# Moving the split weights by 32 bytes in each partition of SBUF

## The reference

```python
proj = h @ w_in[l]
...
x = x + mixed @ w_out[l]
...
up = h @ w_up
...
return (jax.nn.gelu(gate) * val) @ w_down
...
u = h @ w_in
...
y = y + gates[:, :, n] * (branches[n] @ w_branch[n])
return y @ w_out
```

## Time and profile before

| | |
|---|---|
| Median of 3 runs | 3691.65 us |
| Span of the profiled execution | 3692.1 us |
| TensorE matmul busy | 3530.3 us (96%), 28202 matmuls |
| TensorE weight load busy | 3442.9 us (93%) |
| VectorE busy | 2005.9 us (54%) |
| ScalarE busy | 1877.3 us (51%) |
| Mean granted TensorE clock | 0.980 of full speed |
| HBM read | 580.12 MB, 158 GB/s |

### The profile page before, as it was taken

The page is one execution under the profiler, slowest core; times in us unless marked ns, Lnnn a source line. Parts: engine busy times, 40 slices in busy tenths (PEclk is TensorE's granted clock), DMA queues, the critical chain, the costliest instruction groups (busy, mean ns, idle before and its releaser), DMA issues.

```text
span 3692.1 us, 74435 instructions
## 1 busy us (share of the span) xinstructions
PE 3530.3 (96%) x28202; PEld 3442.9 (93%) x28202; DVE 2005.9 (54%) x3133; ACT 1877.3 (51%) x2994; POOL 142.5 (4%) x159
## 2 busy tenths in 40 slices
PE   8999699999999998999999999998999999999999
PEld 7888699999999997899899999998899999999999
DVE  5666445555555545556544555555566644555554
ACT  4444635535534444655545764444565555773443
POOL 0000000000000003000000100000000000110000
PEclk8999899999999998999999999999999999999999
DMA  4223344555555543344345435553434345444554
GB/s 156 103 91 127 109 161 171 182 181 173 182 180 180 182 162 130 121 148 151 130 171 192 173 136 186 188 189 139 140 141 152 135 156 194 171 152 171 184 192 148
DMA packets 89888, 584.03 MB, mean 158 GB/s; under 512 B 10400, under 2 KB 10784, under 8 KB 27552
## 3 DMA queue, kind: packets, MB, share of 16 engines
q1 hardware_dynamic: 88272, 577.54, 44.1%
q0 software_dynamic: 1488, 4.72, 0.4%
HBM read 580.12 MB, written 2.10 MB: 158 GB/s over the span
## 4 chain that ended last, share of the span: by engine, by line
PE 56%; ACT 2%; issue 2%; DVE 1%; DVEq 0%; DMA 0%; ACTq 0%; SPq 0%
PE bank L180 17%; PE bank L182 17%; PE bank L181 17%; PE m L1982 1%; ACT w_hi L156 1%; PE m L1969 1%; PE m L2001 0%; PE m L2010 0%; PE m L234 0%; DVE tn L256 0%; PE m L1984 0%; PE m L2046 0%; PE m L1991 0%; PE m L2012 0%; PE m L2011 0%
## 5 line engine op out<-in xcount | busy, mean ns | idle before, releaser
L161 DVE TENSOR_TENSOR w_lo<-raw,w_hi 128x768 fp32r<-128x768 f32 (+5 forms) x1202 | 1346.4, 1129 | 1047.4 <-ACT w_hi L156 1045.3
L180 PE MATMUL bank<-h,w_hi 128*128 128x256 f32 x5808 | 1677.6, 289 | 45.9 <-DVE h L263 25.4
L181 PE MATMUL bank<-h,w_hi 128*128 128x256 f32 x5808 | 1653.6, 285 | 0.0
L182 PE MATMUL bank<-h,w_lo 128*128 128x256 f32 x5808 | 1653.4, 285 | 0.0
L156 ACT ACTIVATE w_hi<-raw 128x768 fp32r<-128x768 f32 (+5 forms) x1202 | 1107.5, 972 | 167.2 <-PE bank L182 163.7
L180 PEld LDWEIGHTS bank<-h,w_hi 128*128 128x128 f32 x5808 | 1124.8, 194 | 57.3 <-issue 31.6
L181 PEld LDWEIGHTS bank<-h,w_hi 128*128 128x128 f32 x5808 | 1125.9, 194 | 3.0 <-issue 1.4
L182 PEld LDWEIGHTS bank<-h,w_lo 128*128 128x128 f32 x5808 | 1124.7, 194 | 0.0
L180 PE MATMUL bank<-mid,w_hi 128*128 128x256 f32 x1376 | 395.5, 287 | 9.1 <-DVE mid L1930 6.1
L182 PE MATMUL bank<-mid,w_lo 128*128 128x256 f32 x1376 | 386.3, 281 | 0.0
L181 PE MATMUL bank<-mid,w_hi 128*128 128x256 f32 x1376 | 384.9, 280 | 0.0
(11 more groups left out here) (350 smaller groups left out, 3229.7 us busy)
## 6 DMA issues: line engine op xcount, KB each, us to landing
raw<-in_w SPq DMA_DIRECT2D x485, 1024.0 KB, 4.8
raw<-in_w_br SPq DMA_DIRECT2D x96, 512.0 KB, 4.2
raw<-in_w_uq SPq DMA_DIRECT2D x8, 768.0 KB, 4.3
raw<-in_w_ukv SPq DMA_DIRECT2D x8, 512.0 KB, 3.3
bias_t<-in_bias POOLq DMA_DIRECT2D x16, 192.0 KB, 2.9
x<-in_x SPq DMA_DIRECT2D x4, 512.0 KB, 6.5
raw<-in_w_kr SPq DMA_DIRECT2D x4, 512.0 KB, 3.5
out_x<-x SPq DMA_DIRECT2D x1, 2048.0 KB, 6.4
```

The costliest lines, as they stand in the source:

```text
L161: dve.tensor_tensor(w_lo[:, b % 2, c], raw[:, b, c], w_hi[:, b % 2, c].bitcast(F32), ALU.subtract).then_inc(S["lo_done"], 1)
L180: pe.matmul(o, w_hi[:, b % 2, c], a_hi, start=start and k == t0, stop=False)
L181: pe.matmul(o, w_hi[:, b % 2, c], a_lo, start=False, stop=False)
L182: last = pe.matmul(o, w_lo[:, b % 2, c], a_hi, start=False, stop=stop and k == t0 + nt - 1)
```

## The change

Four small tensors are declared that nothing reads or writes. `w_offset` (8 floats, 32 bytes) stands ahead of `w_hi`, `x_offset` (24 floats, 96 bytes) ahead of `x`, and 32 bytes stand ahead of `mixed` and of `mid`. No instruction is added, removed or moved.

```diff
         raw = sb("raw", [4, UNIT])
+        w_offset = sb("w_offset", 8)
         w_hi = sb("w_hi", [2, UNIT], F32R)
         w_lo = sb("w_lo", [2, UNIT], F32R)
+        x_offset = sb("x_offset", 24)
         x = sb("x", [KT, SEQ])
         h = sb("h", [KT, 2 * SEQ], F32R)
...
+        mixed_offset = buf("mixed_offset", 8)
         mixed = buf("mixed", [KT, 2 * SEQ], F32R)
...
+        mid_offset = buf("mid_offset", 8)
         mid = buf("mid", [KT, 2 * SEQ], F32R)
```

## The result

The changed kernel takes 3698.24 us against 3694.03 us for the kernel before (medians of 20 runs each): 1.0015 times, with a 95% interval of 1.0008 to 1.0021. By this ratio it is 0.15% slower, inside what the prediction called no change; 1.2% faster had been forecast. One of the 20 runs of before took 19335.59 us, which nothing here explains; the median does not hang on it. The profiled execution spans 3692.2 us, that of before 3692.1 us, but it is among the faster of its kernel: 3694.61 us, where the 20 runs go from 3693.86 to 3702.94.

The account below looks back on a forecast made before the run. Matmul cost on TensorE was taken to bound the kernel. Savings of 15.2 + 28.2 + 2.1 = 45.5 us, less 0.45 us to the median, took 3692.1 to 3646.1 us, 1.2% faster; range 3624 to 3712 us.

Parts of the forecast that it names:

- What bounds the kernel: Whole kernel: matmuls under way in 96% of the span, so a change in one matmul's cost goes nearly whole into time.
- (a): `h` matmuls, 32 bytes from the weights, fall from 120.0 ns: 15.2 us in feed-forward, 28.2 us elsewhere after the first stage.
- rival 2: Moving operand's own start decides: `h` stays at 120.0 ns, `mixed` and `mid` rise to it, 18 us slower; chance 0.15.
- (b): First stage: cheaper `h` matmuls save 2.1 us, half of the 4.3 us there to be had.
- (c): `mixed` and `mid` matmuls: distance to the weights stays +32 bytes, so 0; bounds 6 us less, 18 us more.
- (d): Weights starting 32 past a multiple of 64 are not dearer by themselves: 0, though up to 3.3 ns could be hidden.
- (e): Splits on ScalarE and VectorE: about 0 from the new alignment, at most 1%, 15 ns, hidden by slack.
- (f): What comes next: loads already keep the faster pace; swapped alignment of small buffers costs 2 us at most either way.
- Rival 1: Buffer's place in memory decides, so 32 bytes change nothing: 3691 to 3692 us; no-change chance 0.20, shared.
- Rival 3: Sign of the distance counts: `h` stays at 120.0 ns (no-change chance 0.20, shared) or reaches 3748 us (0.06).
- rival 4: Weights off a multiple of 64 free more: `h` at 115 ns, 94 us saved, 3598 us; chance 0.06.
- The rule against the change: TensorE's two independent SBUF read ports mean operand distance can't matter, sum 0; no-change chance 0.20, shared.

Follow-up runs that it names:

- r3_h32: Kernel before with 32 bytes put ahead of `h` and 32 behind it, so `h` alone moves up 32 bytes; 3663.49 us, ratio 0.9924.
- r14_d192_again: Second run of the kernel before with 160 bytes of filling, `h`, `mixed` and `mid` starting 192 bytes past the weights; 3595.58 us, ratio 0.9742.
- r1_swap: Kernel before with `h` and the buffer of `mixed` and `mid` exchanging places, weights unmoved; 3664.99 us, ratio 0.9926.
- r6_shift32: Kernel before with 32 bytes ahead of `w_hi` only, so distances between weights and activations stay; 3691.9 us, ratio 1.0.
- r2_swap_h0: Kernel before with `h` and `mixed`/`mid` exchanged and 32 bytes ahead of `h`, putting it at a multiple of 64; 3662.72 us, ratio 0.9926.

## Why the prediction was wrong, step by step

- **What bounds the kernel.** Right. 3.3 ns off each `h` matmul in the traced stretches of `r3_h32` came with 28 us off the time, and up to 6.7 ns off at D 192, `mixed` and `mid` included, with 95 us (`r14_d192_again`: 3690.84 - 3595.58). What a matmul costs from start to start goes into the time.
- **"`h` starts as far from a multiple of 64 bytes as the weights do; `mixed` and `mid` start 32 bytes off."** This is the step that failed. From two distances in the trace, 0 and 32, I made a rule with two classes, same remainder of 64 or not. The rows could not carry the 64: they fit a period of 64, 128, 256 or more alike. The runs give 256, and under it the change takes `h` from 0 to 96, two values with the same 120.0 ns. The addresses in the section on the change, which I had, give the 96: 98560 - 49312. They would not have given a price, since no row has a full-rate matmul at 96 or 160: the rows could not tell that `h` would pay just the 120.0 of before.
- **(a), 43.4 us.** Measured 0, since `h` kept 1377 in 165 us. The size itself was sound where the distance really became 32: `r3_h32` moves `h` to it and leaves the weights alone, and gains 28 us although its `mixed` pays 120.0 where it was read. An estimate: if `mixed` and `mid` pay it throughout, rival 2's reckoning puts that at 18 us, and the two together, 46 us, are near the 45.5 us of the sum.
- **(b)** can't be judged in the changed kernel, where (a) didn't occur, nor well elsewhere: the first `mixed` matmul starts at 444.79 us before, at 443.70 in `r3_h32` and at 446.05 in `r1_swap`, both with `h` at D 32. The 2.1 us is within that spread.
- **(c), 0 for `mixed` and `mid`.** Wrong by 1.9 and 1.0 ns in the traced stretches. I held their distance to be unchanged at 32, but the 96 bytes ahead of `x` and the 32 ahead of `mixed` add up to 128, so D went from 32 to 160. The bounds (6 us less, 18 us more) held what came, about 4 us more between the medians.
- **(d), (e), (f).** Right. `r6_shift32` shows that the weights' start alone costs nothing; the splits moved by 5 ns and 0 ns; the wait for `w_lo` stayed at 14.0 us. One sum beside them was off: at 116.7 ns a stretch of 165 us would hold 165 / 0.1167 + 2 = 1416 `h` matmuls, not the 1408 given as a sign; nothing hangs on it.
- **The rivals.** Rivals 1 and 3 gave the right time, but neither for the right reason. Rival 3's idea, that 32 above and 32 below are different, is true (D 224 costs 118.3, D 32 116.7 in its cheap stretches), but the changed kernel is at 96, not at 224. Rival 1 was struck out by `r3_h32`, rival 2 by `r2_swap_h0`. A price below rival 4's 115 ns does exist, 113.3 at D 64 and 192, but not for weights off a multiple of 64.
- **The rule against the change.** Its consequence, that distance can't matter, gave the right time here without the right reason. What the runs show is 113.3 to 122.2 ns for one instruction when nothing but addresses is changed. The Trainium skill (TensorE: Matmul & The Clock Gate, "Step-by-step: what each phase is for") holds that loading the next weights takes nothing from the running matmul's reads. The runs do not agree with what was drawn from it, that the distance is of no account; whether the two reads get in each other's way, or something else depends on the distance, no run shows.

## What to carry to other kernels

When two buffers show two prices for one instruction, write down their addresses relative to what is read beside them, and ask which periods fit; two points fit many. In a kernel that is bound by back-to-back float32r matmuls, the start of the moving operand against that of the weights is worth a sweep over 256 bytes: 192 bytes of distance gave 2.6% here for 160 bytes of SBUF in each partition. Judge such a version by the times of several executions, and see which of them was profiled, since some distances have two prices.

## What the hardware showed that I had not expected

- The time from start to start of 128 x 128 by 256 float32r matmuls, at a granted clock of 1.00, ran from 113.3 to 122.2 ns when only the places of buffers changed. With one distance for both weights it went with the remainder of 256 of that distance: 119.8 to 120.0 at 0, 113.3 or 117.8 at 64 and 192.
- Absolute place has no part that these runs show: all from the weights on moved by 32 bytes gives a ratio of 1.0 (0.999 to 1.0009), and `h` and `mixmid` exchanged exchange their prices.
- The pace of a dense stretch can differ between executions of one program (here on two chips), 885 against 852 matmuls in the same 100 us, with TensorE busy throughout and the clock at 1.00 in both. Within one execution it can differ between units, 113.5 against 117.8 ns.
- At D 96 and D 0 the average is the same 120.0 ns, though the one has even steps and the other uneven ones: an unchanged average doesn't mean that nothing changed.
